# Four layers on one core: hybrid mixers and output products in one block, the fourth layer's retention beside its input products

## The chip, the cores and the metric

The kernel runs on one core of a Trainium2 chip. The metric is the time of one execution on the device in microseconds (us). The engines of the core are TensorE (PE; its weight loads are shown as PEld), VectorE (DVE), ScalarE (ACT), GpSimd (POOL) and SyncE (SP, which here issues DMAs). PSUM has eight banks of 512 float32 columns for TensorE's results.

## What is computed

Two blocks of two layers each work on 256 tokens of width 1024, in float32. The first two layers mix by convolution, sparse attention, linear attention and a gated MLP. The third layer (`hyb`) runs a gated delta rule and stick-breaking attention side by side, the fourth (`ret`) retention:

```python
def hybrid_mixer(h, ...):
    ...
    o_a = gated_delta_rule(qa, ka, va, g, beta)
    o_a = rms_norm_2(o_a, gdn_norm) * jax.nn.silu(_heads(gate, GDN_HEADS).astype(f32))
    ...
    o_b = stick_breaking_attention(qb, kb, vb)
    o = jnp.concatenate([_merge(o_a), _merge(o_b)], axis=-1).astype(h.dtype)
    return o @ w_out

def retention_mixer(h, w_in, w_out):
    ...
    o = retention_chunkwise(q, k, v)
    o = rms_norm_2(o) * jax.nn.silu(_heads(rg, RET_HEADS).astype(f32))
    return _merge(o).astype(h.dtype) @ w_out
```

Each mixer's result is scaled and added to x; a gated feed-forward part follows in each layer.

## The kernel before

All weights come as one stream of slots of 1 MB (128 partitions x 2048 columns) through a ring of six. SyncE issues the loads in the order of `plan()`. A slot is either modulation weights, which VectorE multiplies by the condition (`mod_sums`, L443), or weights of a product. For a product each float32 weight is split into a high and a low part, in two halves of 1024 columns: ScalarE copies the high part (`split_hi`, L425), VectorE subtracts it for the low part (`split_lo`, L432). The buffers `weights_hi_lo` hold two slots, so a split can begin when the slot two before it has been multiplied. TensorE then does three products for each pair of tiles (high by high, low by high, high by low): 48 products of 256 columns a slot, 24 a half.

Input products (`gemm_phase`, L537) take 15 slots in the hybrid layer and 24 in the fourth. ScalarE takes each finished bank two slots later in its queue (`evac`). Foreign work can be laid between slots: generators for each engine (`beside`) are advanced by one `yield` after each slot, so it all stands in the in-order queues of the engines, behind one split and ahead of the next. Output products (`rows_gemm_phase`, L836) need their activations split too, which GpSimd does (`split_acts`, L763 and L765) into `acts_hi_lo`. `rows_half` (L780) does half a slot of output products by itself; the first two layers use it in their mixers' stage.

An `nc.Block` is a piece of the program; all engines meet where it ends. One block holds layers 0 and 1 and the inputs of layer 2. Then come, each in a block of its own: `hyb_mixers`; the outputs and feed-forward part of layer 2 with the inputs of layer 3; `ret_phase`; the rest.

`hyb_mixers` is a chain of small products with VectorE in between: decays (first their broadcast, L1975), scores, a triangular inverse by doubling (L2014, L2021, L2024), then four steps of the recurrence (L2046 to L2062) with updates on VectorE (L2149 to L2163). The attention's outputs are copied to `oT` by ScalarE (L2229) during the recurrence. The delta outputs are then squared, normed, multiplied by gain and gate (L2169 to L2171), turned (L413) and copied. `ret_phase` computes scores (L2327), multiplies by the decays (L2293), multiplies by the values (L2335, four heads by two token tiles), norms rows of tokens (L2312, L2300), turns 32 blocks (L413) and copies them. The rotations of its q and k run on GpSimd beside the input slots.

## Time and profile before

| | us |
|---|---|
| median of 3 executions | 1613.58 |
| lowest, highest | 1611.7, 1614.3 |
| the profiled execution, its own time | 1613.15 |
| span of its trace, first to last instruction | 1611.4 |

The mean granted TensorE clock over the span is 0.95, as a share of 2.4 GHz: 1.00, or 0.50 for 1.2 GHz. The trace names instructions by line. A float32 product is recorded as two instructions, so 16 products of L2327 stand as x32; the products of split parts and the transposes are recorded once each. "[6.83 <-DVE arena L2171]" is the time that the engine sat idle before the first of these, and what released it. Times of a timeline count from the span's start.

### The profile page before, as it was taken

The numbers are of one execution on the slowest core, as the hardware profiler recorded it, in microseconds if no ns is written. First come the engines' busy times: TensorE is split into PE (matmuls) and PEld (weight loads), VectorE is DVE, ScalarE is ACT, GpSimd is POOL, SyncE is SP. The second block draws the span as 40 slices with busy tenths as digits, with TensorE's granted clock in tenths as the row PEclk, the third lists the DMA queues.
The fourth block names the chain that finished last, engine by engine and source line by source line (L and its number), as shares of the span: only waits on it lengthen the run. The fifth ranks groups of instructions, "written<-read, shape, count | busy, mean of one in ns | idle before, by whom it ended". The sixth has DMA issues, their size and how long they took to land. (4 is left out here: it accounts for less than half of the span.)

```text
span 1611.4 us, 28191 instructions
## 1 busy us (share of the span) xinstructions
PE 1516.3 (94%) x12038; PEld 1485.3 (92%) x12038; DVE 1084.0 (67%) x1451; ACT 750.0 (47%) x1016; POOL 412.4 (26%) x395
## 2 busy tenths in 40 slices
PE   4999899998999999999997879999999997999998
PEld 4999899998998999998997869999999996999998
DVE  7878597796557497796766556776468754465544
ACT  3545465434646365434775234444354443354432
POOL 0123020693121020594001220200329502220022
PEclk9998799998999799998999979999989998999999
DMA  9773389795341469796441004877548771446550
GB/s 395 308 300 139 111 306 343 284 340 203 115 191 63 153 257 360 284 341 221 154 171 43 1 33 147 318 288 262 183 160 294 269 270 53 183 162 218 215 192 27
DMA packets 47212, 336.69 MB, mean 209 GB/s; under 512 B 5360, under 2 KB 5744, under 8 KB 6768
## 3 DMA queue, kind: packets, MB, share of 16 engines
q1 hardware_dynamic: 46224, 333.03, 55.5%
q8 instruction: 95, 1.56, 0.4%
q10 hardware_dynamic: 864, 1.87, 0.3%
q14 instruction: 29, 0.24, 0.0%
HBM read 333.83 MB, written 1.05 MB: 208 GB/s over the span
## 5 line engine op out<-in xcount | busy, mean ns | idle before, releaser
L432 DVE TENSOR_TENSOR weights_hi_lo<-ring,weights_hi_lo 128x1024 fp32r<-128x1024 f32 x426 | 552.3, 1319 | 302.9 <-ACT weights_hi_lo L425 301.8
L425 ACT ACTIVATE weights_hi_lo<-ring 128x1024 fp32r<-128x1024 f32 x426 | 444.4, 1058 | 501.5 <-PE PS L537 277.8
L537 PE MATMUL PS<-hi,weights_hi_lo 128*128 128x256 f32 x3200 | 522.5, 286 | 14.5 <-ACT hi L652 12.4
L537 PEld LDWEIGHTS PS<-hi,weights_hi_lo 128*128 128x128 f32 x3200 | 447.4, 194 | 17.9 <-issue 14.8
L836 PE MATMUL PS<-acts_hi_lo,weights_hi_lo 128*128 128x256 f32 x3264 | 396.4, 284 | 8.2 <-DVE weights_hi_lo L432 8.0
L836 PEld LDWEIGHTS PS<-acts_hi_lo,weights_hi_lo 128*128 128x128 f32 x3264 | 392.8, 191 | 9.3 <-issue 8.6
L763 POOL CAST acts_hi_lo<-arena 128x256 fp32r<-128x256 f32 x144 | 135.6, 942 | 835.7 <-PE PS L836 419.9
L537 PE MATMUL PS<-lo,weights_hi_lo 128*128 128x256 f32 x1600 | 324.7, 285 | 0.0
L443 DVE CUSTOM_DVE_ANT_0 ring<-ring,cond 128x1024 f32<-128x1024 f32 x192 | 253.6, 1359 | 0.0
L537 PEld LDWEIGHTS PS<-lo,weights_hi_lo 128*128 128x128 f32 x1600 | 251.4, 193 | 0.0
L537 PE MATMUL PS<-weights_hi_lo,hi 128*128 128x256 f32 x1248 | 203.5, 285 | 1.2 <-ACT hi L652 1.2
L537 PEld LDWEIGHTS PS<-weights_hi_lo,hi 128*128 128x128 f32 x1248 | 172.0, 189 | 3.1 <-issue 2.9
L765 POOL TENSOR_TENSOR acts_hi_lo<-arena,acts_hi_lo 128x256 fp32r<-128x256 f32 x144 | 168.7, 1171 | 11.5
L537 PE MATMUL PS<-weights_hi_lo,lo 128*128 128x256 f32 x624 | 125.9, 283 | 0.0
L537 PEld LDWEIGHTS PS<-weights_hi_lo,lo 128*128 128x128 f32 x624 | 97.0, 190 | 0.0
L609 PEld LDWEIGHTS PS<-constS,arena 128*128 128x128 f32 x384 | 62.8, 254 | 12.7 <-ACT arena L644 11.8
L609 PE MATMUL PS<-constS,arena 128*128 128x1 f32 x384 | 63.2, 292 | 10.7 <-ACT arena L644 9.9
L2187 POOL TENSOR_TENSOR arena<-arena,constS 128x1024 f32<-128x1024 f32 x6 | 12.3, 2062 | 146.6 <-DVE arena L2115 136.5
L652 ACT ACTIVATE hi<-spare,mods 128x256 fp32r<-128x256 f32 x64 | 31.7, 507 | 31.1 <-DVE spare L663 31.1
L644 ACT ACTIVATE arena<-X 128x512 f32<-128x512 f32 (+1 forms) x40 | 21.7, 545 | 45.1 <-PE PS L609 22.0
L780 PE MATMUL PS<-acts_hi_lo,weights_hi_lo 128*128 128x256 f32 x288 | 39.7, 299 | 2.3 <-DVE heads L1592 2.1
L780 PEld LDWEIGHTS PS<-acts_hi_lo,weights_hi_lo 128*128 128x128 f32 x288 | 38.0, 205 | 2.9 <-DVE heads L1592 2.5
(349 smaller groups left out, 1117.9 us busy)
## 6 DMA issues: line engine op xcount, KB each, us to landing
ring<-in_stream_dram SPq DMA_DIRECT2D x313, 1024.0 KB, 4.9
constS<-in_const_dram SPq DMA_DIRECT2D x1, 1856.0 KB, 8.6
cond<-in_rows_dram SPq DMA_DIRECT2D x2, 512.0 KB, 5.2
arena<-in_x_dram ACTq DMA_DIRECT2D x1, 1024.0 KB, 11.3
smallS<-in_small_dram SPq DMA_DIRECT2D x1, 883.0 KB, 13.4
out_dram<-arena ACTq DMA_DIRECT2D x2, 256.0 KB, 2.5
out_dram<-arena SPq DMA_DIRECT2D x2, 256.0 KB, 3.3
constS<-in_const_dram SPq DMA_DIRECT2D x1, 320.0 KB, 14.7
```

The source lines that it names most:

```text
L425: act.activation(wsp[:, g % 2, 0, at:at + HALF], ring[:, n % RING, at:at + HALF], ACT.Copy).then_inc(*ready.one())
L432: dve.tensor_tensor(wsp[:, g % 2, 1, at:at + HALF], ring[:, n % RING, at:at + HALF], wsp[:, g % 2, 0, at:at + HALF].bitcast(F32), ALU.subt ...
L443: ins = dve.tensor_tensor_reduce(w[:, r, :], w[:, r, :], cond[:, 0 if q < 12 else 1, :], 1.0, 0.0, ALU.mult, ALU.add, mods[:, q, k:k + 1])
L537: mm = pe.matmul(o, lhs, rhs, start=k + g + j == 0, stop=k == KD - 1 and j == 2, skip_group_check=True)
L609: mm = pe.matmul(PS[:, bank, m:m + 1], sq[:, u % 2, c * SEQ + m * P:c * SEQ + (m + 1) * P], ones[:, 0:1], start=u + c + m == 0, stop=u == ...
L644: act.activation(sq[:, u % 2, 0:len(tiles) * SEQ], X[:, tiles[0]:tiles[-1] + 1, :].rearrange("p k t -> p (k t)"), ACT.Square).then_inc(*xs ...
L652: act.activation(hi[:, k, :], tmp[:, k % 4, :], ACT.Identity, bias=mods[:, q, k:k + 1]).then_inc(*hd.one())
L763: pool.tensor_copy(asp[:, a % 2, 0, g, :], src).then_inc(*acts_hi.one())
L765: pool.tensor_tensor(asp[:, a % 2, 1, g, :], src, asp[:, a % 2, 0, g, :].bitcast(F32), ALU.subtract).then_inc(*acts_lo.one())
L780: mm = pe.matmul(y_of(k), w[:, g, k * P:(k + 1) * P], x[:, g, :], start=fresh and g + j == 0 and (k % 2 == 0 or k == KD - 1), stop=False, ...
L836: mm = pe.matmul(y_of(k), w[:, g, k * P:(k + 1) * P], x[:, g, :], start=fresh and i + g + j == 0 and (k % 2 == 0 or k == KD - 1), stop=i = ...
L2187: pool.tensor_tensor(CT[v % 2], LT, cst(f"level{v}").unsqueeze(1).broadcast_to((P, 8, P)), ALU.mult).then_inc(*ctd.one())
```

## The change

1. `hyb_mixers` runs in the block of the inputs, and waits for single signals of the inputs' stage instead of the block's end. Its buffers are laid out anew: matrices of the triangular inverse and the decayed keys lie in idle halves of `weights_hi_lo`, in the order in which they come free for splits.
2. The hybrid layer's output slots come in the order 4, 6, 0, 2 (attention rows first). The first two are multiplied in `hyb_mixers` by `rows_half`, three halves ahead of the turns of the delta outputs and the fourth behind them, into banks 0 to 4. The first two turned blocks are split by ScalarE and VectorE straight from PSUM. The output phase goes on with the other two slots.
3. `ret_phase` is gone. Scores, decays, the products with the values, the norm and the gate are generators beside the fourth layer's input slots. The products with the values are done the other way round (channels on partitions), so nothing has to be turned. For the norm VectorE adds squares to one tile, TensorE sums it by a column of ones and spreads the roots. Gates are kept for two slots only and multiplied at once. The inputs use three banks instead of four, and the first output slot's weights are split in the inputs' stage (`split_weights=True`).
4. All of it is one block.

`split_hi` and `split_lo` take an argument for the halves to do. In the diff `slots` are the first two output slots, `following` the third.

```diff
-    return [("rows", name, i, k, 0) for k in ((4, 6, 0, 2) if kind == "mix" else range(0, chunks, 2))]
+    return [("rows", name, i, k, 0) for k in ((4, 6, 0, 2) if kind != "ret" else range(0, chunks, 2))]
...
+        if kind == "hyb":
+            phases.append((("mixed", l), merge(outs[:2], ("mixed", l))))
+            outs = outs[2:]
...
+            split_at = [[SPLIT_AT + 2 * SLOT * (product_no[n] % 2) + HALF * i for i in range(4)] for n in slots]
+            (hi0, hi1, lo0, lo1), (next_hi0, next_hi1, _, next_lo1) = split_at
+            decT, LT, T_, U_, W_ = (area(a, 8, P) for a in (7184, 8208, 9232, 10256, 11280))
+            CT = [area(a, 8, P) for a in (hi0, hi1)]
+            kbT, vb, kg, kdec, egb = (area(a, 8, P) for a in (lo0, lo1, next_hi0, next_hi1, next_lo1))
...
+                pe.wait_ge(*tka.at(4))
+                rows_half(pe, slots[0], 0, y_of, fresh=True)
+                rows_half(pe, slots[0], 1, y_of, fresh=True)
+                rows_half(pe, slots[1], 0, y_of, fresh=False)
+                pe.wait_ge(*onr.at(1))
+                transposes(pe, lambda i: og[:, i % 2, i // 2 * P:i // 2 * P + P], 8, 6, ft)
+                rows_half(pe, slots[1], 1, y_of, fresh=False)
...
+                exponents(4)
+                split_lo(dve, slots[0], (0,))
+                dve.wait_ge(*up_.at(1))
+                split_lo(dve, slots[0], (1,))
+                dve.wait_ge(*wp_.at(1))
+                dve.tensor_copy(wT, bank2(4)).then_inc(*wts.one())
...
+                            dve.wait_ge(*sts.at(n + 1))
+                            split_lo(dve, slots[1], (n - 1,))
...
+                split_lo(dve, following[0])
+                dve.wait_ge(*ft.at(1))
+                dve.wait_ge(acts_hi.sem, 2 * last + 2)
+                for g in range(2):
+                    dve.tensor_tensor(asp[:, last % 2, 1, g, :], PS[:, 6, g * SEQ:(g + 1) * SEQ],
+                                      asp[:, last % 2, 0, g, :].bitcast(F32), ALU.subtract).then_inc(*acts_lo.one())
...
+                for i in range(2):
+                    split_acts(pool, oT[:, 4 + 2 * i:6 + 2 * i, :], slots[i:i + 1], ready=[tka.at(3 + i)] * 2)
...
+                split_hi(act, slots[0], (0,))
+                act.wait_ge(*up_.at(1))
+                act.activation(u, bank2(2), ACT.Copy).then_inc(*us.one())
+                split_hi(act, slots[0], (1,))
+                for g in range(2):
+                    act.wait_ge(*dif.at(4 * g + 4))
+                    act.activation(Zs[g], Zs[g], ACT.Exp).then_inc(*av.one())
+                act.wait_ge(*wp_.at(1))
+                split_hi(act, slots[1], (0,))
+                for b in range(2):
+                    if b:
+                        act.wait_ge(*kvs.at(3))
+                        split_hi(act, slots[1], (1,))
...
+                split_hi(act, following[0])
+                act.wait_ge(*ft.at(1))
+                act.wait_ge(acts_lo.sem, 2 * last)
+                for g in range(2):
...
+                if i >= 18:
+                    act.wait_ge(*gated.at(i - 17))
+                return act.activation(gates[:, i % 2, :], bank, ACT.Silu)
...
+                gemm_phase(blk, ("proj", l), lambda i: 256 if 8 <= i < 16 else 0, evac, banks=3, split_weights=True,
+                           beside=retention(QK, V, gates))
+            return proj, None, QK
...
+            score_at, out_at = {10: 0, 12: 1, 13: 2, 15: 3}, {12: 0, 14: 1, 18: 2, 19: 3}
...
+            def pe_beside(pe):
+                for i in range(24):
+                    if i in score_at:
+                        h = score_at[i]
+                        pe.wait_ge(*rot_done.at(h + 5))
+                        if h:
+                            pe.wait_ge(*at_.at(h))
                         for kt in range(TT):
                             for c in range(2):
+                                mm = pe.matmul(PS[:, 3, 256 * kt:256 + P * kt], QK[:, 8 + 2 * h + c, kt * P:(kt + 1) * P],
                                                QK[:, 2 * h + c, kt * P:SEQ], start=c == 0, stop=c == 1)
                         mm.then_inc(*ap_.one())
+                    if i in out_at:
+                        h = out_at[i]
+                        pe.wait_ge(*at_.at(h + 1))
+                        pe.wait_ge(*taken.at(10 + 2 * h))
+                        if h >= 2:
+                            pe.wait_ge(*yn.at(2 * h - 2))
+                        o = pair_banks(h)
+                        for c in range(4):
+                            for kt in range(TT):
+                                mm = pe.matmul(o[:, c, kt * P:SEQ], V[:, kt, h * 512 + c * P:h * 512 + (c + 1) * P],
+                                               att[:, h, 256 * kt:256 + P * kt], start=kt == 0 and c % 2 == 0, stop=kt == 1,
+                                               skip_group_check=True)
                         mm.then_inc(*op.one())
+                    if i in (16, 21):
+                        g = 0 if i == 16 else 1
+                        pe.wait_ge(*at_.at(4))
+                        if g:
+                            pe.wait_ge(*yn.at(4))
+                        for h in (2 * g, 2 * g + 1):
+                            pe.wait_ge(*ad.at(h + 1))
+                            for m in range(TT):
+                                mm = pe.matmul(PS[:, 3, 2 * (h % 2) + m:2 * (h % 2) + m + 1], sq[:, h % 2, m * P:(m + 1) * P],
+                                               ones[:, 0:1], start=h % 2 + m == 0, stop=True, skip_group_check=True)
+                        mm.then_inc(*gsum.one())
+                    if i in (17, 22):
+                        g = 0 if i == 17 else 1
+                        pe.wait_ge(*grc.at(g + 1))
+                        for j in range(4):
+                            mm = pe.matmul(PS[:, 3, j * P:(j + 1) * P], r[:, 4 * g + j:4 * g + j + 1].to_broadcast((P, P)), ident,
+                                           start=j == 0, stop=True, skip_group_check=True)
+                        mm.then_inc(*gsp.one())
+                    yield
+            def act_beside(act):
+                for i in range(25):
+                    for h, at in ((0, 14), (1, 16), (2, 20), (3, 21)):
+                        if i == at:
+                            act.wait_ge(*op.at(h + 1))
+                            if h:
+                                act.wait_ge(*ad.at(h))
+                            if h >= 2:
+                                act.wait_ge(*yn.at(4))
+                            for b in range(2):
+                                act.activation(squares(h, b), pair_banks(h)[:, 2 * b:2 * b + 2, :], ACT.Square).then_inc(*gsq.one())
+                    if i in (17, 22):
+                        g = 0 if i == 17 else 1
+                        act.wait_ge(*gsum.at(g + 1))
+                        act.activation(r[:, 4 * g:4 * g + 4], PS[:, 3, 0:4], ACT.Sqrt, bias=cst("eps"), scale=1.0 / 512).then_inc(*grt.one())
+                    if i in (18, 23):
+                        act.wait_ge(*gsp.at(1 if i == 18 else 2))
+                        act.activation(sq[:, 0, :], PS[:, 3, :], ACT.Copy).then_inc(*rsb.one())
+                    yield
...
+            def dve_beside(dve, order):
+                for i in range(28):
+                    for h, at in ((0, 11), (1, 13), (2, 14), (3, 16)):
+                        if i == at:
+                            dve.wait_ge(*ap_.at(h + 1))
+                            dve.tensor_tensor(att[:, h, :], PS[:, 3, 0:384], dec[:, h, :], ALU.mult).then_inc(*at_.one())
+                    for h, at in ((0, 14), (1, 16), (2, 20), (3, 21)):
+                        if i == at:
+                            a, b = squares(h, 0), squares(h, 1)
+                            dve.wait_ge(*gsq.at(2 * h + 2))
+                            order(dve.tensor_tensor(a, a, b, ALU.add))
+                            dve.tensor_tensor(a[:, 0, :], a[:, 0, :], a[:, 1, :], ALU.add).then_inc(*ad.one())
+                    if i in (17, 22):
+                        g = 0 if i == 17 else 1
+                        dve.wait_ge(*grt.at(g + 1))
+                        dve.reciprocal(r[:, 4 * g:4 * g + 4], r[:, 4 * g:4 * g + 4]).then_inc(*grc.one())
+                    if i in (18, 23):
+                        g = 0 if i == 18 else 1
+                        dve.wait_ge(*rsb.at(g + 1))
+                        dve.wait_ge(*ap_.at(4))
+                        for h in (2 * g, 2 * g + 1):
+                            for b in range(2):
+                                v = sq[:, 0, h % 2 * 256:h % 2 * 256 + 256].unsqueeze(1).broadcast_to((P, 2, SEQ))
+                                dve.tensor_tensor(yT[:, 4 * h + 2 * b:4 * h + 2 * b + 2, :], pair_banks(h)[:, 2 * b:2 * b + 2, :], v,
+                                                  ALU.mult).then_inc(*yn.one())
+                    n = i - 19
+                    if 0 <= n < 8:
+                        dve.wait_ge(*taken.at(17 + n))
+                        dve.wait_ge(*yn.at(n + 1))
+                        v = yT[:, 2 * n:2 * n + 2, :].rearrange("p k t -> p (k t)")
+                        dve.tensor_tensor(v, v, gates[:, n % 2, :], ALU.mult).then_inc(*gated.one())
+                    yield
...
+            inputs, mixers, mixed = layers[2]
+            inputs(blk)
+            mixers(blk)
+            outputs(blk, 2, mixed, acts_split=1, acts_ready=[state.pop("mixed")] * 4, fresh=False, y_banks=(0, 1, 2, 3, 4))
+            ffn_phases(blk, 2)
+            layers[3][0](blk)
+            outputs(blk, 3, layers[3][2], acts_ready=state.pop("gated"))
```

TensorE at the end of the hybrid layer, before (L2046 to L2062 are the recurrence's last step, L413 the turns, L836 the output products, L609 sums of the next norm; a branch ends a block or phase):

```order
L2046 MATMUL PS<-arena 64x128 x4
L2050 MATMUL PS<-arena 64x128 x4
L2062 MATMUL PS<-arena 64x128 x4
L413 MATMUL PS<-constS,arena 128x128 x8
L1932 UNCONDITIONAL_BRANCH
L815 UNCONDITIONAL_BRANCH
L836 MATMUL PS<-acts_hi_lo,weights_hi_lo 128x256 x192
L609 MATMUL PS<-constS,arena 128x1 x16
```

And of the change (L2077 to L2093 are the last step, L786 `rows_half`, L416 the turns, L846 the output phase, L615 the next norm):

```order
L2077 MATMUL PS<-arena 64x128 x4
L2081 MATMUL PS<-arena 64x128 x4
L2093 MATMUL PS<-heads 64x128 x4
L786 MATMUL PS<-acts_hi_lo,weights_hi_lo 128x256 x72
L416 MATMUL PS<-constS,arena 128x128 x8
L786 MATMUL PS<-acts_hi_lo,weights_hi_lo 128x256 x24
L823 UNCONDITIONAL_BRANCH
L846 MATMUL PS<-acts_hi_lo,weights_hi_lo 128x256 x96
L615 MATMUL PS<-constS,arena 128x1 x16
```

72 output products stand ahead of the turns and 24 behind them; one branch is gone.

VectorE between the inverse and the recurrence's state updates, before (L2088 exponents of the attention, L2141 the copy of w, L2149 and L2152 values of v, L2159 and L2163 state updates):

```order
L2088 TENSOR_TENSOR heads<-heads,PS 128x384 x2
L2088 TENSOR_TENSOR spare<-spare,PS 128x384 x2
L2141 COPY arena<-PS 128x1024
L2088 TENSOR_TENSOR spare<-spare,PS 128x384 x2
L2149 COPY arena<-arena 64x4x128
L2159 COPY arena<-PS 128x512
L2152 TENSOR_TENSOR arena<-arena,PS 64x4x128
L2163 SCALAR_TENSOR_TENSOR arena<-arena,PS 128x128 x4
L2152 TENSOR_TENSOR arena<-arena,PS 64x4x128
```

And of the change (L2124, L2180, L2188, L2191, L2198 and L2202 are the same work, L438 is `split_lo`):

```order
L2124 TENSOR_TENSOR spare<-spare,PS 128x384 x2
L438 TENSOR_TENSOR weights_hi_lo<-ring,weights_hi_lo 128x1024 x2
L2180 COPY arena<-PS 128x1024
L2124 TENSOR_TENSOR spare<-spare,PS 128x384 x2
L2188 COPY heads<-arena 64x4x128
L2198 COPY arena<-PS 128x512
L2191 TENSOR_TENSOR heads<-arena,PS 64x4x128
L2202 SCALAR_TENSOR_TENSOR arena<-arena,PS 128x128 x4
L438 TENSOR_TENSOR weights_hi_lo<-ring,weights_hi_lo 128x1024
L2191 TENSOR_TENSOR heads<-arena,PS 64x4x128
```

Two split pieces now stand ahead of the copy of w, and one behind the state update shown (one more behind the next).

ScalarE at the end of the fourth layer's inputs, before (L2248 takes a gate's bank, L2312 and L408 are `ret_phase`; the splits, L425, stand between the rows of L2248):

```order
L2248 ACTIVATE arena<-PS 128x2x256 x3
L2421 UNCONDITIONAL_BRANCH
L2307 UNCONDITIONAL_BRANCH
L2312 ACTIVATE arena,stat<-PS 128x512 x4
L408 ACT_TABLE_LOAD
L408 ACTIVATE stat<-stat 128x4
L2312 ACTIVATE arena,stat<-PS 128x512 x4
```

And of the change (L429 is `split_hi`, L2314 takes a gate's bank, L2415 are the roots, L2418 the copy of the spread roots):

```order
L2415 ACT_TABLE_LOAD
L2415 ACTIVATE stat<-PS,constS 128x4
L429 ACTIVATE weights_hi_lo<-ring 128x1024 x2
L2314 ACT_TABLE_LOAD
L2314 ACTIVATE arena<-PS 128x512
L2418 ACTIVATE arena<-PS 128x512
L2314 ACTIVATE arena<-PS 128x512
L429 ACTIVATE weights_hi_lo<-ring 128x1024 x2
L2314 ACTIVATE arena<-PS 128x512
L869 UNCONDITIONAL_BRANCH
L429 ACTIVATE weights_hi_lo<-ring 128x1024 x16
```

The roots and the copy stand between splits, and the split of the first output slot stands behind the last bank but one.

VectorE at the same place, before (L432 is `split_lo`, L2293 the decays of `ret_phase`):

```order
L457 TENSOR_TENSOR mods<-mods,smallS 128x8
L432 TENSOR_TENSOR weights_hi_lo<-ring,weights_hi_lo 128x1024 x2
L2421 UNCONDITIONAL_BRANCH
L2287 UNCONDITIONAL_BRANCH
L2293 TENSOR_TENSOR arena<-PS,constS 128x384 x4
L400 TENSOR_SCALAR stat<-stat 128x4
```

And of the change (L462 and L463 end a modulation, L438 is `split_lo`, L2448 multiplies by the roots, L2455 by the gates):

```order
L462 SCALAR_TENSOR_TENSOR mods<-mods,smallS 128x8
L463 TENSOR_TENSOR mods<-mods,smallS 128x8
L438 TENSOR_TENSOR weights_hi_lo<-ring,weights_hi_lo 128x1024 x2
L2448 TENSOR_TENSOR arena<-PS,arena 128x512 x4
L2455 TENSOR_TENSOR arena<-arena 128x512
L438 TENSOR_TENSOR weights_hi_lo<-ring,weights_hi_lo 128x1024 x2
L2455 TENSOR_TENSOR arena<-arena 128x512 x3
L888 UNCONDITIONAL_BRANCH
L438 TENSOR_TENSOR weights_hi_lo<-ring,weights_hi_lo 128x1024 x16
```

Four root products and a gate product stand between the split of the last input slot and that of the first output slot.

## Rows read from the trace of the kernel before

**Rows 1.** Page, part 1: busy time, share of the span, instructions.

```profile
PE 1516.3 (94%) x12038; PEld 1485.3 (92%) x12038; DVE 1084.0 (67%) x1451; ACT 750.0 (47%) x1016; POOL 412.4 (26%) x395
```

**Rows 2.** Windows; PE, PEld, DVE, ACT, POOL busy; clock; DMA share; GB/s.

```profile
947.10:960.00 12.90, 1.97 (x8) 1.59 (x9) 8.25 (x10) 5.21 (x6) 2.60 (x4) 0.57 0.00 1
960.00:985.60 25.60, 25.60 (x195) 25.60 (x195) 14.78 (x16) 8.84 (x10) 9.98 (x13) 0.88 0.53 192
1329.60:1359.90 30.30, 21.16 (x88) 14.47 (x89) 12.75 (x22) 12.77 (x27) 2.59 (x4) 0.92 0.00 1
```

**Rows 3.** PE timeline, fourth layer (start us, us, what, idle before, its releaser).

```profile
1328.46 0.40 PE L537 MATMUL PS<-weights_hi_lo,lo 128*128 128x256 f32 x2
...
1329.18 0.40 PE L537 MATMUL PS<-weights_hi_lo,lo 128*128 128x256 f32 x2
...
1330.58 5.48 PE L2327 MATMUL PS<-arena 128*128 128x256 f32 x32 [1.00 <-PEq L2421]
...
1335.89 10.47 PE L2335 MATMUL PS<-arena 128*128 128x512 f32 x24
...
1359.91 48.09 PE L836 MATMUL PS<-acts_hi_lo,weights_hi_lo 128*128 128x256 f32 x384 [3.86 <-DVE weights_hi_lo L432]
```

**Rows 4.** The same timeline, hybrid layer's mixers and its output products.

```profile
861.45 2.03 PE L1975 MATMUL PS<-constS,stat 128*128 128x128 f32 x16
...
953.91 1.97 PE L413 MATMUL PS<-constS,arena 128*128 128x128 f32 x8 [6.83 <-DVE arena L2171]
...
960.00 25.61 PE L836 MATMUL PS<-acts_hi_lo,weights_hi_lo 128*128 128x256 f32 x192 [4.12 <-DVE weights_hi_lo L432]
```

**Rows 5.** ScalarE's timeline, from the hybrid inputs to its output products.

```profile
859.18 0.60 ACT L1721 ACTIVATE arena<-PS 128x512 f32<-128x512 f32 x1 [4.10 <-PE PS L537]
...
926.85 1.02 ACT L2223 ACTIVATE arena<-PS 128x1024 f32<-128x1024 f32 x1 [6.81 <-PE PS L2031]
...
944.36 0.60 ACT L2229 ACTIVATE arena<-PS 128x512 f32<-128x512 f32 x1 [4.69 <-PE PS L1967]
...
965.56 1.06 ACT L425 ACTIVATE weights_hi_lo<-ring 128x1024 fp32r<-128x1024 f32 x1 [4.36 <-PE PS L836]
```

**Rows 6.** VectorE's timeline, end of the hybrid layer's recurrence and its norm.

```profile
928.64 1.23 DVE L2141 COPY arena<-PS 128x1024 f32<-128x1024 f32 x1 [3.02 <-PE PS L2034]
929.78 1.15 DVE L2088 TENSOR_TENSOR spare<-spare,PS 128x384 f32<-128x384 f32 x2
930.84 0.41 DVE L2149 COPY arena<-arena 64x512 f32<-64x512 f32 x1
...
945.24 0.69 DVE L2152 TENSOR_TENSOR arena<-arena,PS 64x512 f32<-64x512 f32 x1 [2.27 <-PE PS L2046]
...
952.63 1.22 DVE L2171 TENSOR_TENSOR arena<-arena 128x1024 f32<-128x1024 f32 x1
```

**Rows 7.** GpSimd's timeline, splits of activations beside output products.

```profile
960.39 1.39 POOL L763 CAST acts_hi_lo<-arena 128x256 fp32r<-128x256 f32 x1
...
961.86 1.59 POOL L765 TENSOR_TENSOR acts_hi_lo<-arena,acts_hi_lo 128x256 fp32r<-128x256 f32 x1
```

**Rows 8.** VectorE's timeline, a modulation piece and a split, fourth layer's inputs.

```profile
1314.58 1.22 DVE L443 CUSTOM_DVE_ANT_0 ring<-ring,cond 128x1024 f32<-128x1024 f32 x1
...
1319.19 1.23 DVE L432 TENSOR_TENSOR weights_hi_lo<-ring,weights_hi_lo 128x1024 fp32r<-128x1024 f32 x1 [0.58 <-ACT weights_hi_lo L425]
```

**Rows 9.** Timelines: sums by a column, table change, four multiplies of 512.

```profile
747.33 0.95 PE L609 MATMUL PS<-constS,arena 128*128 128x1 f32 x8
...
1342.28 1.28 ACT L408 ACT_TABLE_LOAD   x1 [0.28 <-DVE stat L400]
...
1347.89 2.73 DVE L2300 SCALAR_TENSOR_TENSOR arena<-PS,stat,arena 128x512 f32<-128x512 f32 x4
```

**Rows 10.** Waits of PE, second layer, 450 to 600 us: total, times, longest.

```profile
PE PS L780 <- DVE heads L1592: 1.2, 1, 1.2
```

**Rows 11.** Windows again, columns as in Rows 2, first layer's mixers.

```profile
150.00:154.00 4.00, 4.00 (x21) 3.94 (x19) 4.00 (x7) 2.42 (x3) 4.00 (x1) 0.52 0.79 276
```

717 lines of the change are left out of this document (336 added, 381 removed).

## Prediction

> **What bounds the kernel now.** I read the page first: TensorE is busy 94% of the span [rows 1], so time can only come from stretches in which it idles, runs at half clock, or does work that could go. The windows by stretch show two such places, one in each of the last two layers. After the hybrid layer's recurrence TensorE works 1.97 us out of 12.90 at a mean granted clock of 0.57, and the output products behind it start at the lower level (mean 0.88) [rows 2]. In the fourth layer 30.3 us lie between the input products and the output products, with DMA at rest [rows 2]. TensorE's own timeline then says what ended each wait.
>
> Pace: six of the large products start 0.72 us apart [rows 3], so 0.12 us each at 2.4 GHz, a slot of 48 takes 5.76 us and half a slot 2.88.
>
> **Part 1, the hybrid layer.** Where TensorE stood before, in order of time.
>
> (a) The broadcasts of g stand behind a block boundary and start at 861.45 [rows 4]. In the new order there is no boundary. The broadcasts wait only for the last bank to be taken, by the ScalarE copy that starts at 859.18 and takes 0.60 [rows 5], so they start near 859.85. VectorE's masks of the decays wait for TensorE's transposes behind these broadcasts, so the whole stage moves: gain 1.6.
>
> (b) Two split pieces are put into VectorE's queue ahead of the copy of w (L2141). VectorE's second piece waits for ScalarE's: ScalarE copies u from 926.85 to 927.87, then splits 1.06, to 928.95 [rows 5]; VectorE then needs 1.23 [rows 8], to 930.2. Behind it stand the copy of w, two exponents and the copy of v, which before began at 928.64 and ended at 931.25 [rows 6]: 2.6 us, now from 930.2 to 932.9. The recurrence waits for just these: loss 1.7. The other two pieces go into VectorE's waits between the state updates, 2.27 us where I see one [rows 6], and cost 1.23: hidden, if ScalarE's half is there.
>
> (c) Recurrence to output products. Before: the recurrence's last product ends at 947.08 (953.91 - 6.83), TensorE waits 6.83 for the norm, the gain and the gate on VectorE (to 953.85), turns eight blocks in 1.97, waits 4.12 for a boundary and a first split, then does 192 products in 25.61 [rows 4, 6]. Now three halves, 72 products of 8.64 us, need no delta output. Their weights are split in (b); their activations are attention copies, the last of which ScalarE ends at 944.96 [rows 5]. GpSimd splits them at no more than 1.4 and 1.6 us a piece [rows 7], four pieces a slot: the second slot's are there by 951 and wanted from 952.7 on. So the 6.83 is covered by products, with 1.8 to spare; the turns, at full clock, take about half of 1.97; the fourth half (2.88) covers the copy and split of the turned blocks, two ScalarE and two VectorE pieces. Gains: 6.83 (the wait), 4.12 (the boundary and the first split), 1.0 (the turns at full clock), and 25.61 - 192 x 0.12 = 2.6 (the products at full clock).
>
> Sum of part 1: 1.6 - 1.7 + 6.8 + 4.1 + 1.0 + 2.6 = **14.4**.
>
> **Part 2, the fourth layer.** Removed from TensorE's path: all from the end of the inputs (1330.58 - 1.00 = 1329.58) to the first output product (1359.91), 30.3 us [rows 3], and the half-clock start of 384 output products, 48.09 - 46.08 = 2.0 [rows 3].
>
> Added to TensorE between input slots, one after the other with them:
> - scores, the same 16 products: 1335.89 - 1330.58 = 5.3 [rows 3];
> - outputs turned, 16 products of 256 and 16 of 128 columns. Before they were 12 of 512 in 10.47: 6144 columns both times, so 10.5 [rows 3];
> - sums of squares by a column of ones, eight products: four take 0.95, so 1.9 [rows 9];
> - spreading the roots, eight products of 128: the same shape takes 2.03 for eight, so 2.0 [rows 4].
> Gone without replacement: 32 transposes, the row-wise norm, the barrier and the cold split. Sum added 19.7.
>
> Waits: the rest is laid beside 24 slots. VectorE gets four decays, four pairs of adds, eight multiplies by the root and eight by the gate: at 0.69 each at most, some 18 us in a stage that TensorE lengthens by 19.7. Each of these stands in VectorE's or ScalarE's queue behind one split and ahead of the next, so a late one delays the next slot's weights. I followed the queues slot by slot and find one place where the lead runs out. Count from the end of slot 22. TensorE spreads the roots (1.0), and does slot 23 until 6.8. VectorE has just done a modulation piece (2 x 1.22 and small ones) and slot 23's split (2 x 1.23), and is free at 2.2 [rows 8]. It then owes four multiplies (2.73 [rows 9]), to 4.9, and a gate (0.69), to 5.6. ScalarE may take bank 22 only after that gate, since there are two gate buffers: 6.2. Then it splits the next weights, first half to 7.3, and VectorE the low part to 8.5. TensorE wants them at 6.8: 1.7, with semaphore hops 2.0. For all other places I take 0.5 in all: in the second layer, built in the same way, TensorE's longest wait for such a piece is 1.2 [rows 10]. Bounds for all waits: 0 to 8.
>
> Gain of part 2: 30.3 + 2.0 - 19.7 - 2.5 = **10.1** (bounds 4.6 and 12.6).
>
> ScalarE changes tables in that chain, for the root and back for the gate's Silu. A change takes 1.28 here [rows 9], and at that both are done before TensorE or VectorE could wait for them longer than I have counted. The Trainium skill, "ScalarE: Activation LUTs", section "Table sets: the hidden batching unit", gives about 2.7 us for one; by that the last stall would grow by up to 2 x 1.4 and the forecast be some 1592. The row decides.
>
> Extra DMA or semaphores: the stream has the same slots, in another order for the hybrid outputs; DMA runs at 192 GB/s beside the output products [rows 2] and is not pressed. The ring's prefetch is hidden by TensorE's full slots before and behind.
>
> **Sum.** 14.4 + 10.1 = 24.5 off the profiled execution's 1613.15 gives 1588.6; that execution lies 0.4 under the median of 1613.58, so 1589.
>
> **Rivals.**
> (R1) Only the hybrid layer gains. The queues of the fourth layer lose at several slots what the pause cost: some 10 us in 14 slots, 0.7 each. For it: nearly every slot from 10 on has a piece of foreign work, and VectorE waits in its queue for TensorE's result each time. Against: the second layer's waits [rows 10]. Time: 1613.6 - 14.4 = 1599. Chance 0.11.
> (R2) Slower. In-order queues lose their one-slot lead at every slot from 10 to 23, and TensorE then sees ScalarE's and VectorE's split in full, 1.06 + 1.23 = 2.3, 14 times: 32 us. Part 2 is then 12.6 - 32 = -19.6, the whole 14.4 - 19.6 = -5.2: 1619. It decides from stalls of 27 us in all, 1.9 a slot. Against: the pieces beside one slot are well under the 5.76 of it. Chance 0.03.
> (R3) The clock falls where I count full pace. After the wait of 6.8 it was at half. But it also stood at 0.52 from 150 to 154 us, when TensorE was busy 4.00 of 4.00 us with thin products of 64 columns [rows 11]. The new sums (one column) and the 1.7 of (b) are such places: three of them, at 2.6 each as in the outputs, give 1597. Chance 0.12. The Trainium skill, "TensorE: Matmul & The Clock Gate", section "HAM oscillation — how this bites in real kernels", ties the fall to pauses of TensorE; by that rule only (b) could be hit, 1591.6, and the fourth layer would keep its clock. The row at 150 us shows a fall without a pause, so I keep this case.
> (R4) The change doesn't do what it says in the hybrid layer: the three halves wait for GpSimd's splits or the banks, so the products stay behind the norm. Then the 6.8 stays: 1596. Against: by the durations in (c) both slots' pieces are there before they are wanted. Chance 0.06.
> (R5) Better than forecast: (b) and the stalls hidden, 1589 - 4 = 1585. It lies inside the forecast's own range.
>
> **How the numbers follow.** Forecast 0.68, with its own range of 1583 to 1594 (R5's end, and waits of 7 instead of 2.5). The range that should hold 8 in 10 reaches up over R3, R4 and R1, and down to 1582, where a 14.4 of 16 and a 10.1 of 13 or more would be needed: 1582 to 1600. A measurement of this kernel tells about 0.2% (3 us) from no change. All cases but R2 are faster by more. Faster 0.95, same 0.02, slower 0.03.
>
> **What would show it.** Right: no idle of TensorE over 1 us between the recurrence's last product and the hybrid layer's next norm, and its clock at 1.00 there; recurrence about as late as before; the fourth layer's output products start within 3 us of the last input product, at clock 1.00; input stage about 22 us longer. Wrong: product waits for split weights at slots 11 to 23, or a clock of 0.50 in the input stage of the fourth layer or behind the copy of w; a wait of the fourth half for the turned blocks. What would make the sum wrong most is a queue order in VectorE that I took to be covered.

## The result and the profile after

The changed kernel takes **1589.4 us** (median of 1586.94, 1589.38 and 1593.05) against 1613.25 for the kernel before (median of four). The ratio of the means is 0.9855, 95% interval 0.983 to 0.9881, or 23.4 us less. Two executions in a slower state of the chip are left out here and below: one of the changed kernel (1671.7 us at a mean granted clock of 0.82; with it the median is 1591.2) and one of the kernel before (2130.4 us at 0.64). Two more series of the same kernel, further down, gave ratios of 0.983 (0.9812 to 0.9848) and 0.9835 (0.9815 to 0.9855). All eleven times lie between 1582.7 and 1593.1 with a median of 1586.9, against a median of 1613.1 for 34 of the kernel before: 26 us less. The prediction was 1589, 24.5 less, in a range of 1582 to 1600.

That spread of 10 us is the first thing to explain, and one stretch of the profile turns out to account for about half of it. The profile is of the slowest of these executions (1593.05, span 1591.2). First TensorE's timeline from the hybrid layer's inputs to its next norm (start in us, us, what, idle before and what ended it), which answers to [rows 4]. Here L2003 is the broadcast of g, L2086 and L2077 to L2093 the recurrence (with the attention's products, L1990, laid between), L786 the halves of the output products, L416 the turns, L846 the rest of the products:

```profile
860.19 2.02 PE L2003 MATMUL PS<-constS,stat 128*128 128x128 f32 x16 [0.43 <-ACT arena L1731]
...
930.71 1.13 PE L2086 MATMUL PS<-heads,arena 64*128 64x128 f32 x8 [2.35 <-DVE heads L2188]
...
933.52 1.97 PE L2077 MATMUL PS<-arena 128*64 128x128 f32 x8
935.28 1.91 PE L2081 MATMUL PS<-arena 128*64 128x128 f32 x8
...
950.82 1.04 PE L2081 MATMUL PS<-arena 128*64 128x128 f32 x8
...
952.80 8.78 PE L786 MATMUL PS<-acts_hi_lo,weights_hi_lo 128*128 128x256 f32 x72
961.42 1.04 PE L416 MATMUL PS<-constS,arena 128*128 128x128 f32 x8
962.21 3.08 PE L786 MATMUL PS<-acts_hi_lo,weights_hi_lo 128*128 128x256 f32 x24
965.12 11.52 PE L846 MATMUL PS<-acts_hi_lo,weights_hi_lo 128*128 128x256 f32 x96
976.48 4.36 PE L615 MATMUL PS<-constS,arena 128*128 128x1 f32 x32
```

Behind the recurrence everything is as forecast: no row has a wait in brackets. The 6.83 and the 4.12 of [rows 4] are gone, the turns take 1.04 instead of 1.97, and from the recurrence's end to the norm's first sum it is 23.7 us (952.80 to 976.48) where it was 38.4 (947.08 to 985.45). Inside the recurrence something is wrong: the same four products (eight rows of L2081) take 1.91 us at 935 and 1.04 at 951. The windows name it (busy time of PE, PEld, DVE, ACT, POOL; granted clock; DMA share; GB/s):

```profile
931.00:945.00 14.00, 14.00 (x71) 12.02 (x70) 3.73 (x7) 2.29 (x3) 0.40 (x1) 0.53 0.10 40
...
953.00:962.00 9.00, 9.00 (x78) 9.00 (x78) 7.55 (x8) 4.55 (x5) 0.16 (x1) 1.00 0.13 54
962.00:976.00 14.00, 14.00 (x121) 14.00 (x119) 7.96 (x12) 6.54 (x9) 4.20 (x4) 1.00 0.53 183
```

For 14 us TensorE works without a pause at its lower level, 1.2 GHz, behind a wait of 2.35 us. From the first product of the recurrence to the first half it takes 22.09 us; at full clock, as we shall see, 15.61. So this execution pays 6.48 us there. VectorE's timeline shows where the 2.35 come from, and answers to [rows 6] (L438 are the low parts of split weights, L2180 the copy of w, L2188 the copy of v; two exponents lie between):

```profile
923.56 1.22 DVE L438 TENSOR_TENSOR weights_hi_lo<-ring,weights_hi_lo 128x1024 fp32r<-128x1024 f32 x1
926.95 1.23 DVE L438 TENSOR_TENSOR weights_hi_lo<-ring,weights_hi_lo 128x1024 fp32r<-128x1024 f32 x1 [2.17 <-ACT weights_hi_lo L429]
928.09 1.22 DVE L2180 COPY arena<-PS 128x1024 f32<-128x1024 f32 x1
...
930.15 0.41 DVE L2188 COPY heads<-arena 64x512 f32<-64x512 f32 x1
...
958.43 1.23 DVE L2212 TENSOR_TENSOR arena<-arena 128x1024 f32<-128x1024 f32 x1
```

The second piece waits for ScalarE and holds back the copy of w. The last row is the gate behind the norm: it ends at 959.66, and TensorE comes to the turns only at 961.42, so the halves cover the chain with 1.8 us to spare, as predicted.

The fourth layer, from the scores (L2365) over outputs (L2377), sums of squares (L2389) and spreads (L2396) to the output products (L846); what lies between are input products. It answers to [rows 3]:

```profile
1259.90 1.47 PE L2365 MATMUL PS<-arena 128*128 128x256 f32 x8
1261.20 2.78 PE L2377 MATMUL PS<-later,arena 128*128 128x256 f32 x16
...
1327.24 0.95 PE L2389 MATMUL PS<-constS,arena 128*128 128x1 f32 x8
...
1333.76 1.05 PE L2396 MATMUL PS<-constS,stat 128*128 128x128 f32 x8
...
1341.61 45.69 PE L846 MATMUL PS<-acts_hi_lo,weights_hi_lo 128*128 128x256 f32 x384 [1.09 <-DVE weights_hi_lo L438]
1387.14 4.91 PE L615 MATMUL PS<-constS,arena 128*128 128x1 f32 x32
```

and the windows there (the first holds the whole stage behind its start, the second the output products):

```profile
1200.00:1341.00 141.00, 140.51 (x1152) 139.06 (x1150) 100.33 (x116) 62.92 (x78) 64.34 (x51) 1.00 0.65 240
1341.00:1387.00 46.00, 45.39 (x383) 45.42 (x384) 27.77 (x28) 18.67 (x20) 15.54 (x24) 1.00 0.54 197
```

Of a gap of 30.3 us one wait of 1.09 is left, at full clock. The span is 20.2 us shorter: the first of the next norm's sums comes 9.0 us earlier in the hybrid layer (976.48 against 985.45), of which 0.9 are lost again ahead of the fourth layer (its inputs start 8.1 us earlier, 1181.99 against 1190.07; in the 23.5 us from the first sum on the granted clock was 0.78 against 0.85). The fourth layer gains 12.6, and some 0.5 is lost behind it.

### The profile page after: what moved, and what is told of

Read it like the earlier page. It is cut to its first block, busy times and chain, and to the rows that moved or that the text cites. A ratio compares the mean times of both kernels' runs of the same rounds, so it can differ in the third digit from the quotient of the medians.

```text
span 1591.2 us, 28263 instructions
## 1 busy us (share of the span) xinstructions
PE 1513.8 (95%) x12078; PEld 1487.8 (94%) x12078; DVE 1086.8 (68%) x1461; ACT 750.8 (47%) x1011; POOL 406.1 (26%) x391
## 4 chain that ended last, share of the span: by engine, by line
PE 74%; issue 11%; POOL 8%; DVE 5%; ACT 1%; DMA 0%; ACTq 0%; POOLq 0%; DVEq 0%
PE PS L543 44%; PE PS L846 14%; POOL acts_hi_lo L769 4%; POOL acts_hi_lo L771 4%; PE PS L786 3%; PE PS L615 2%; DVE ring L449 2%; PE PS L1078 1%; PE PS L2377 1%; PE PS L1456 1%; PE PS L623 1%; PE PS L2055 1%; PE PS L1436 1%; DVE weights_hi_lo L438 1%; PE PS L1464 1%
## 5 line engine op out<-in xcount | busy, mean ns | idle before, releaser
L438 DVE TENSOR_TENSOR weights_hi_lo<-ring,weights_hi_lo 128x1024 fp32r<-128x1024 f32 x426 | 550.9, 1317 | 272.8 <-ACT weights_hi_lo L429 271.4
L429 ACT ACTIVATE weights_hi_lo<-ring 128x1024 fp32r<-128x1024 f32 x426 | 444.5, 1058 | 477.4 <-PE PS L543 270.1
L543 PE MATMUL PS<-hi,weights_hi_lo 128*128 128x256 f32 x3456 | 562.2, 285 | 14.1 <-ACT hi L658 12.1
L543 PEld LDWEIGHTS PS<-hi,weights_hi_lo 128*128 128x128 f32 x3456 | 480.5, 193 | 17.5 <-issue 14.6
L846 PE MATMUL PS<-acts_hi_lo,weights_hi_lo 128*128 128x256 f32 x3168 | 379.8, 281 | 1.3 <-DVE weights_hi_lo L438 1.1
L846 PEld LDWEIGHTS PS<-acts_hi_lo,weights_hi_lo 128*128 128x128 f32 x3168 | 376.4, 189 | 2.0 <-issue 1.3
L543 PE MATMUL PS<-lo,weights_hi_lo 128*128 128x256 f32 x1728 | 349.8, 284 | 0.0
L543 PEld LDWEIGHTS PS<-lo,weights_hi_lo 128*128 128x128 f32 x1728 | 270.6, 193 | 0.0
L543 PE MATMUL PS<-weights_hi_lo,hi 128*128 128x256 f32 x992 | 162.5, 286 | 1.2 <-ACT hi L658 1.2
L543 PEld LDWEIGHTS PS<-weights_hi_lo,hi 128*128 128x128 f32 x992 | 137.2, 190 | 3.1 <-issue 2.9
L543 PE MATMUL PS<-weights_hi_lo,lo 128*128 128x256 f32 x496 | 100.0, 283 | 0.0
L543 PEld LDWEIGHTS PS<-weights_hi_lo,lo 128*128 128x128 f32 x496 | 77.2, 190 | 0.0
L615 PEld LDWEIGHTS PS<-constS,arena 128*128 128x128 f32 x384 | 62.0, 251 | 12.5 <-ACT arena L650 11.6
L615 PE MATMUL PS<-constS,arena 128*128 128x1 f32 x384 | 62.4, 290 | 10.7 <-ACT arena L650 9.9
L786 PE MATMUL PS<-acts_hi_lo,weights_hi_lo 128*128 128x256 f32 x384 | 50.9, 293 | 2.0 <-DVE heads L1602 2.0
L786 PEld LDWEIGHTS PS<-acts_hi_lo,weights_hi_lo 128*128 128x128 f32 x384 | 48.8, 198 | 2.6 <-DVE heads L1602 2.4
```

The lines of the kernel that those rows point to most:

```text
L429: act.activation(wsp[:, g % 2, 0, at:at + HALF], ring[:, n % RING, at:at + HALF], ACT.Copy).then_inc(*ready.one())
L438: dve.tensor_tensor(wsp[:, g % 2, 1, at:at + HALF], ring[:, n % RING, at:at + HALF], wsp[:, g % 2, 0, at:at + HALF].bitcast(F32), ALU.subt ...
L543: mm = pe.matmul(o, lhs, rhs, start=k + g + j == 0, stop=k == KD - 1 and j == 2, skip_group_check=True)
L615: mm = pe.matmul(PS[:, bank, m:m + 1], sq[:, u % 2, c * SEQ + m * P:c * SEQ + (m + 1) * P], ones[:, 0:1], start=u + c + m == 0, stop=u == ...
L786: mm = pe.matmul(y_of(k), w[:, g, k * P:(k + 1) * P], x[:, g, :], start=fresh and g + j == 0 and (k % 2 == 0 or k == KD - 1), stop=False, ...
L846: mm = pe.matmul(y_of(k), w[:, g, k * P:(k + 1) * P], x[:, g, :], start=fresh and i + g + j == 0 and (k % 2 == 0 or k == KD - 1), stop=i = ...
```

## The experiments

Each run stood beside runs of the kernel before on its own chip, and three chips were used. "Less" and "more" with an interval come from the ratio of the means to the kernel before on the same chip; a plain difference of medians can lie some 3 us away from it. Four things were to be settled: what each part gives alone; whether the half clock in the recurrence comes from the longer wait; whether the cover of the norm is what gains in the hybrid layer; and what the last wait in the fourth layer is.

**The same kernel again** (two runs, on two chips). No edit.

> The changed kernel once more, unaltered, as the ruler for the others on this chip. Theory A (the clock falls in the recurrence in some executions only, as its profile had it at 0.53 over 931 to 945 us for about 6.4 us): times from about 1585 to 1593, scattered over several us, and the profile shows the recurrence either from 930.7 to about 946.4 at 1.00 or to 952.8 at half clock. Theory B (the clock always falls there, since the waits ahead of it are always the same): the recurrence ends 22 us after it began in this profile too, and the times lie around 1590 with the scatter of the kernel before, some 2.5 us.

Measured: 1584.8 (1582.7 to 1587.4). Its profile has the same wait, but a short fall:

```profile
928.09 1.13 PE L2086 MATMUL PS<-heads,arena 64*128 64x128 f32 x8 [2.35 <-DVE heads L2188]
...
931.58 1.91 PE L2081 MATMUL PS<-arena 128*64 128x128 f32 x8
...
945.32 8.79 PE L786 MATMUL PS<-acts_hi_lo,weights_hi_lo 128*128 128x256 f32 x72
```

The recurrence takes 17.23 us (928.09 to 945.32), 1.62 over full pace, instead of 6.48: neither of the two ends that the expectation named, but between them. Theory A in kind: the fall's length changes from one execution to the next with the program unchanged. That it can be nothing was not seen.

> The changed kernel unaltered, beside the next three on one chip. From its seven undisturbed times so far (1582.7 to 1593.1): a median between 1584 and 1590, with a spread of 4 us or more. If the half clock in the recurrence comes and goes, the profile shows it again at another length than the 14 and the 4 us seen so far, or not at all.

Measured: 1586.9 (1583.6 to 1589.2); recurrence 17.23 again (932.93 to 950.16). The expected spread is there. The spread of the times is not all from this place: in this profile the broadcast of g starts 3.6 us later than in the one before (860.56 against 856.95), so something ahead of it moves too.

**The parts alone.** The fourth layer's functions of the kernel before put into the changed one, and the reverse:

```
-            layers[3][0](blk)
-            outputs(blk, 3, layers[3][2], acts_ready=state.pop("gated"))
+            layers[3][0](blk)
+        layers[3][1]()
+        with block() as blk:
+            outputs(blk, 3, layers[3][2])
```

> Part one of the change alone: the hybrid layer as changed, the fourth layer's retention in a block of its own behind its inputs, as before. By the sum of the prediction 14.4 us less than the kernel before (about 1599), with the clock at half through the recurrence 6 less gained, 8 to 9 us (about 1604). If the parts add up, it stands 10 to 12 us above the changed kernel in the same runs.

Measured: 1600.4 (1590.1 to 1602.7, six times), ratio 0.991 (0.9886 to 0.9934): 14.5 us less (10.6 to 18.4). It stands 12.9 above the changed kernel on the same chip by the ratios, 15.7 by the medians, where 10 to 12 were expected. Its profile, of the slowest of the six, has the long fall: wait of 2.34, recurrence of 22.09 (930.38 to 952.47).

> Part two of the change alone: the hybrid layer as in the kernel before, the fourth layer's retention beside its inputs as changed. By the sum of the prediction 10.1 us less than the kernel before; by the profile of the changed kernel, whose only wait there is 1.1 us where 2.5 were put down, 11 to 12 less, so about 1601 to 1603. Rival (the parts help each other, since one block of the program is left between them less): clearly under 10, with the rest only where both are there.

Measured: 1601.5 (1600.5 to 1601.8), ratio 0.9925 (0.9913 to 0.9937): 12.1 us less (10.2 to 14.0). The parts add up within these intervals: 14.5 + 12.1 = 26.6, against 26 for the whole over all series. The rival in which they help each other, with part two clearly under 10, is out. So is, with its interval, the case that only the hybrid layer gains. This kernel has the recurrence of the kernel before with its wait of 1.07, and its profile shows that a short fall can come there too:

```profile
932.46 1.13 PE L2058 MATMUL PS<-arena 64*128 64x128 f32 x8 [1.07 <-DVE arena L2152]
...
934.53 1.90 PE L2049 MATMUL PS<-arena 128*64 128x128 f32 x8
936.22 1.91 PE L2053 MATMUL PS<-arena 128*64 128x128 f32 x8
938.06 1.16 PE L2058 MATMUL PS<-arena 64*128 64x128 f32 x8
```

**The split pieces late.** VectorE's side only:

```
-                split_lo(dve, slots[0], (0,))
-                dve.wait_ge(*up_.at(1))
-                split_lo(dve, slots[0], (1,))
...
                             dve.tensor_copy(new, kv).then_inc(*sts.one())
+                            split_lo(dve, slots[0], (0,))
...
-                            split_lo(dve, slots[1], (n - 1,))
+                            split_lo(dve, slots[n - 1], (2 - n,))
...
                 dve.tensor_tensor(og, og, GT, ALU.mult).then_inc(*onr.one())
+                split_lo(dve, slots[1], (1,))
```

> VectorE's pieces of the split move out of the stretch ahead of the recurrence: the first output slot's two go behind the first and second state update, the second slot's first behind the third, its last behind the gated outputs. ScalarE's side stays. The wait of TensorE ahead of the recurrence should fall from 2.35 us to about 1.1, as in the kernel before. Theory A (the longer wait brought the clock down for the recurrence): 1.3 us from the wait and up to 6.4 from the clock, so 2 to 8 us less than the changed kernel, about 1583 to 1588, with the recurrence at 1.00. Theory B (the clock falls at the phase that the stage has by then, whatever this wait is): only about 1.3 us less, and the recurrence at 0.5 all the same. Rival: the moved pieces come too late for the fourth half or for the next slot, and 1 to 2 us come back there as waits.

Measured: 1584.2, four times within 1583.8 to 1585.3.

```profile
932.03 1.13 PE L2086 MATMUL PS<-heads,arena 64*128 64x128 f32 x8 [1.07 <-DVE heads L2185]
...
934.10 1.09 PE L2077 MATMUL PS<-arena 128*64 128x128 f32 x8
935.03 1.04 PE L2081 MATMUL PS<-arena 128*64 128x128 f32 x8
...
947.64 8.79 PE L786 MATMUL PS<-acts_hi_lo,weights_hi_lo 128*128 128x256 f32 x72
```

The wait is 1.28 shorter, as wanted, the recurrence runs at full pace in 15.61 us, and no late piece makes TensorE wait behind it. The median, though, is only 0.5 under the changed kernel on the same chip (1584.8, with the short fall in its profile), so the 2 to 8 us of theory A did not come. The four times spread by 1.5 us against 4.8, but that is not shown to be the edit's doing: the two kernels below that have the late pieces and one more edit each, in the fourth layer or at the block's end, spread by 8.9 and 6.7.

**The wait filled.** Eight products of the unit matrix, which nobody reads:

```
                 later_sums(6)
+                for _ in range(8):
+                    pe.matmul(PS[:, 0, 0:P], ident, ident, start=True, stop=True)
                 pe.wait_ge(*wts.at(1))
```

> The changed kernel with eight 128x128 fp32 products of the unit matrix, whose result nobody reads, put into bank 0 ahead of TensorE's wait for the recurrence: at 0.22 us each they fill 1.8 of its 2.35 us and delay nothing. Theory A (the clock fell because TensorE stood idle there): the recurrence runs at 1.00, up to 6.4 us less than the changed kernel where that has the fall, median 2 to 6 less; the wait shown is 0.5. Theory B (the fall has another cause, earlier in the stage): no change in time within 1 us, and the recurrence at 0.5 as before.

Measured: 1588.4 (1581.1, 1588.2, 1588.5, 1588.8). Theory A wanted a median 2 to 6 us less; it is 3.6 more than the changed kernel's on this chip. The profile is of the fastest, 1581.1, and there the recurrence is as theory A has it, with VectorE's work unchanged and the wait down to 0.56:

```profile
926.73 1.95 PE L2069 MATMUL PS<-constS 128*128 128x128 f32 x16
929.23 1.13 PE L2088 MATMUL PS<-heads,arena 64*128 64x128 f32 x8 [0.56 <-DVE heads L2190]
...
944.85 8.78 PE L786 MATMUL PS<-acts_hi_lo,weights_hi_lo 128*128 128x256 f32 x72
```

15.62 us. But the three other times are all above the changed kernel's highest there (1587.4), and no trace says where they lost it. As a remedy this is not shown.

**The wait lengthened.** The kernel with the late pieces, with the copy of w made three times:

```
                 dve.wait_ge(*wp_.at(1))
+                order(dve.tensor_copy(wT, bank2(4)))
+                order(dve.tensor_copy(wT, bank2(4)))
                 dve.tensor_copy(wT, bank2(4)).then_inc(*wts.one())
```

> The kernel with the late pieces (1584.2), and VectorE makes its copy of w three times instead of once, which only lengthens TensorE's wait ahead of the recurrence, from 1.07 to about 3.5 us (2 x 1.22). Theory A (the longer wait brings the clock down for the recurrence): 2.4 from the wait and 1.5 to 6.4 from the clock, so 4 to 9 us more, and half clock in the recurrence in the profile. Theory B (the order of the pieces, not the wait, made the difference): 2.4 us more, with the recurrence at 1.00.

Measured: 1594.2 (1580.6 to 1597.8, six times), 10.0 over the median of the kernel with the late pieces on another chip. The wait itself grew by 2.37. The fall is in the profile:

```profile
926.00 1.78 PE L2086 MATMUL PS<-heads,arena 64*128 64x128 f32 x8 [3.44 <-DVE heads L2187]
...
931.36 1.90 PE L2081 MATMUL PS<-arena 128*64 128x128 f32 x8
933.19 1.16 PE L2086 MATMUL PS<-heads,arena 64*128 64x128 f32 x8
```

It costs 3.23 us there (18.84 from 926.00 to 944.84). So theory B's recurrence at 1.00 is out for this execution; but three of seven profiles with the wait of 1.07 have a short fall too (table below), so one profile doesn't show that the length of the wait brought it. The profiled execution is at the same time the fastest of the six. Its granted clock was 1.00 from 876 to 892, where the changed kernel has 0.79 to 0.85, which can be why. The times don't decide either: the medians leave 7.6 over the wait, the ratios (0.9868 with 0.9838 to 0.9897, against 0.9827 with 0.9811 to 0.9842) leave 4.2 with an uncertainty of some 5, and the five slower executions have no trace. Theory A is likely, not shown.

**More filling**, here and at the norms, on the kernel with the late pieces and the early split (below):

```
+                        if h0 < 6:
+                            for _ in range(7):
+                                pe.matmul(PS[:, 2, 0:P], ident, ident, start=True, stop=True)
                         pe.wait_ge(*dif.at(h0))
```

> The kernel with the late pieces and the early split in the fourth layer (1581.9 on another chip), and idle products of the unit matrix (128x128 fp32, 0.22 us each) in three waits of the hybrid stage: seven in each of the two of 1.80 us ahead of the later sums, four in the 1.07 us ahead of the recurrence. Theory A (TensorE's idle time there brings the clock down in the recurrence): no half clock between 905 and 960 us, the scatter of the times stays under 3 us, and the median 0 to 2 us under that kernel. Theory B (the falls come from further ahead in the program): falls and scatter as before, and a median within 1 us of it. Rival: the seven take longer than the wait, and 0.5 to 1 us is lost.

Measured: 1584.8 (1580.6 to 1586.1), 2.1 under the changed kernel on this chip. Its base is on another chip; against the kernel before the two have 0.9824 and 0.9817, so no gain over it is seen. Full clock from 905 to 960 us in the profile, as theory A has it (15.61 for the recurrence), and still a spread of 5.5 in the times, as theory B has it. Clock falls elsewhere (0.87 from 876 to 892 in this profile) may make it; which place makes it was not traced.

```
                     unit_sums(pe, u, sq, 0, xsq, xsum)
+                for _ in range(3):
+                    pe.matmul(PS[:, 1, 0:P], ident, ident, start=True, stop=True)
                 spread(pe, r, 2, xr, rx)
+                for _ in range(5):
+                    pe.matmul(PS[:, 1, 0:P], ident, ident, start=True, stop=True)
```

> The same kernel as base (1581.9 on another chip), and idle products of the unit matrix beside every norm of X: three (0.7 us at full clock) in the wait for the root, five (1.1) in the wait for the first scaled tile. In the profiles the input products behind each norm run at half clock for some 5 us, which costs about half of that at each of eight places. If the idle 0.6 and 1.2 us are what brings the clock down: half clock goes from the first products of each stage, up to 8 x 2.7 = 21 us less. If the thin sums ahead of them (32 products of one column, in which TensorE counts as busy) have brought it down by then: the fillers run at half clock themselves, take 0.44 us each, 3.5 us together against the 1.8 idle, and 8 x 1 to 1.7 = 8 to 13 us are lost.

Measured: 1584.2 (1582.2 to 1587.5). Neither 21 gained nor 8 lost. The norm behind the hybrid layer, first without, then with the fillers (L617 sums, L645 and L648 fillers, L625 spread, L543 input products):

```profile
970.26 3.95 PE L617 MATMUL PS<-constS,arena 128*128 128x1 f32 x32
...
976.67 1.19 PE L543 MATMUL PS<-hi,weights_hi_lo 128*128 128x256 f32 x4 [1.21 <-ACT hi L660]
...
982.86 0.63 PE L543 MATMUL PS<-hi,weights_hi_lo 128*128 128x256 f32 x4
```

```profile
972.13 4.87 PE L617 MATMUL PS<-constS,arena 128*128 128x1 f32 x32
976.86 1.63 PE L645 MATMUL PS<-constS 128*128 128x128 f32 x6
978.28 1.06 PE L625 MATMUL PS<-constS,stat 128*128 128x128 f32 x4
979.13 2.27 PE L648 MATMUL PS<-constS 128*128 128x128 f32 x10
981.13 0.75 PE L543 MATMUL PS<-hi,weights_hi_lo 128*128 128x256 f32 x4
...
984.80 0.63 PE L543 MATMUL PS<-hi,weights_hi_lo 128*128 128x256 f32 x4
...
988.07 0.73 PE L543 MATMUL PS<-hi,weights_hi_lo 128*128 128x256 f32 x4 [0.97 <-DVE weights_hi_lo L438]
```

At this norm the input products do start at full clock now, 0.75 for four against 1.19. The fillers ahead of them ran at half clock. From the first sum to the thirty-first product it is 12.60 us without and 12.67 with, but the sums, which stand ahead of all fillers, took 0.92 of that more in this execution (4.87 against 3.95): behind the sums 0.85 is gained. The stage, faster at its start, then waits 0.97 for VectorE's split, which the slow start had covered. So it goes at three norms that both traces show: from the first sum to the second slot's first product it is 14.71, 15.05 and 15.24 us without fillers and 15.94, 15.38 and 15.06 with them, and at the second of these the first four products are still at half clock (1.20). What the fillers gain, the wait for the split takes back.

**Turns first**, on the kernel with the late pieces: the wait for the gated outputs and the turns ahead of all four halves, so that nothing covers the norm.

```
+                pe.wait_ge(*onr.at(1))
+                transposes(pe, lambda i: og[:, i % 2, i // 2 * P:i // 2 * P + P], 8, 6, ft)
                 rows_half(pe, slots[0], 0, y_of, fresh=True)
```

> The kernel with the late pieces (1584.2), and the turns of the delta outputs put ahead of all four halves of the output products, so that nothing covers the norm's chain. If the cover is worth what the prediction says: TensorE waits 6.8 us for the gated outputs, and the clock at half for some us after it adds 1 to 3, so 7 to 10 us more, 1591 to 1594. Rival (the products fit in later at no loss, because something else is late): under 3 us more.

Measured: 1593.2 (1591.6 to 1595.2), 9.0 more than the median of its base on another chip. The traces say the same: from the recurrence's end to the norm's first sum it is 32.78 us (948.18 to 980.96) against 23.70 (947.64 to 971.34), 9.1 more.

```profile
955.10 1.94 PE L416 MATMUL PS<-constS,arena 128*128 128x128 f32 x8 [6.92 <-DVE arena L2210]
956.69 13.07 PE L786 MATMUL PS<-acts_hi_lo,weights_hi_lo 128*128 128x256 f32 x96
```

The wait is back with 6.92, the turns are at half clock, and so is the start of the products (13.07 for 96, where 72 and 24 took 8.79 and 3.08). That is the cover's price: the wait and 2.1 of clock.

**The block's end back** between the hybrid inputs and the delta stage, on the kernel with the late pieces.

```
             inputs(blk)
+        with block() as blk:
             mixers(blk)
```

> The kernel with the late pieces (1584.2), and the end of the block put back between the hybrid layer's input products and its delta stage, as in the kernel before. By the prediction's term this is worth 1.6 us, so 1585 to 1586, and in the profile 1.6 us more from the end of the input products to the broadcast of the gates' sums. Rival: nothing (under 0.5), because the stage would wait for the norm of the heads anyway.

Measured: 1585.0 (1584.1 to 1590.9), too near to tell by times. In the profile the broadcast starts 2.02 us after the start of the last two input products (860.98 to 863.00), 1.18 without the boundary (859.74 to 860.92): 0.84, neither the 1.6 of the term nor nothing. In the kernel before it is 2.70 (858.75 to 861.45), so from before to after 1.52 are gained. What made that kernel's boundary 0.68 dearer was not tried; it also had SyncE's wait for the layer's tables in it.

```profile
862.56 0.36 PE L1998 MATMUL PS<-stat,constS 128*128 128x8 f32 x2 [1.19 <-PEq L2520]
```

**The fourth layer's split first**, on the kernel with the late pieces:

```
+                if name == ("proj", 3):
+                    split_hi(act, following[0])
                 take(n_pe - 2)
```

> The kernel with the late pieces (1584.2), and in the fourth layer ScalarE splits the first output slot's weights ahead of its evacuation of the gate's seventh bank, which waits for a gate buffer. If that evacuation is what holds the split back, TensorE's wait of 1.09 us ahead of the fourth layer's output products goes, 1.1 us less, about 1583, which the profile can show and the times hardly. Rival (VectorE's own order holds it, which has the normed heads to write ahead of its half of the split): the wait stays between 0.5 and 1.1.

Measured: 1581.9 (1580.3, 1581.4, 1581.9, 1582.9, 1589.2), ratio to before 0.9817 (0.9798 to 0.9837). The wait is gone; first TensorE, then VectorE:

```profile
1330.92 14.25 PE L848 MATMUL PS<-acts_hi_lo,weights_hi_lo 128*128 128x256 f32 x119
```

```profile
1328.45 0.68 DVE L2456 TENSOR_TENSOR arena<-arena 128x512 f32<-128x512 f32 x1
1329.05 2.35 DVE L438 TENSOR_TENSOR weights_hi_lo<-ring,weights_hi_lo 128x1024 fp32r<-128x1024 f32 x2
```

VectorE splits right behind the gate, since ScalarE's half is there; before, it stood idle 1.67 us at this point for it. So ScalarE's order was the cause, and VectorE's own order was not. The kernel has the lowest median of all here, 1581.9, but its interval overlaps the changed kernel's, and the two never ran on the same chip.

All profiles of the recurrence together, from its first product to the first half (in the two kernels with the old order, to its end):

```
wait ahead   recurrence, us                    over full pace
0.17, 0.56   15.61, 15.62                      0, 0
1.07         15.6 or 15.7 four times,          0, 0, 0, 0,
             17.3, 17.23, 17.23                1.6, 1.6, 1.6
2.34, 2.35   22.09, 22.09, 17.23, 17.23        6.5, 6.5, 1.6, 1.6
3.44         18.84                             3.2
```

A short fall of 1.6 came with either wait; the long one was seen only behind 2.34 and 2.35, in two of four. Not every wait brings a fall: TensorE also waits twice for 1.80 us earlier in the stage (L1979), and the granted clock was 1.00 from 905 to 928 us in all three profiles of the changed kernel.

## Why the prediction came out right, and where it was off

The time was forecast for mostly the right reasons. Two errors offset each other, and that they did is luck: a fall of the clock in the hybrid layer that the sum left out, and a fourth layer that gained more than forecast.

**Part 1.** Forecast 14.4; alone it gave 14.5, with an interval of 8 us, so the terms must be read in the traces.
- (a) 1.6: the way from the last input products to the broadcast is 1.52 shorter. Right in size; the block's end by itself cost 0.84 where it was put back, and what the other 0.68 was stays open.
- (b) -1.7: the wait grew by 1.28 (2.35 against 1.07). The size is right. What the step left out is the clock behind it: the mean extra time in the recurrence is 4.0 us in four profiles of this order, 0.7 in seven of the shorter wait. This is the term that failed, -1.7 where in the first profile 1.28 + 6.48 = 7.8 were lost and in the next two 1.28 + 1.62 = 2.9. That the longer wait causes the long fall is the likeliest reading of the table, but these are few profiles, and no series of times shows it.
- (c) 6.83 + 4.12 + 1.0 + 2.6 = 14.5: the way from the recurrence's end to the norm is 38.37 - 23.68 = 14.7 shorter. Right, and the turns put first (9.1 back in the traces) show that the cover is the cause of most of it. The rest, the 4.12 of boundary and first split and what is left of the clock, was not taken out by itself.
- The two other pieces, called hidden: at 940.39 and 948.79 in VectorE's waits, at no cost. Right.

Sum by traces: 1.5 - 1.3 + 14.7 = 14.9 without a fall, 8.4 with the long one, 13.3 with the short one.

**Part 2.** Forecast 10.1 (bounds 4.6 and 12.6); alone 12.1 (10.2 to 14.0). By the profile, from the first input product to the first output product it is 169.84 us before (1190.07 to 1359.91) and 159.62 after (1181.99 to 1341.61), 10.2 less, and the output products are 2.4 shorter (47.93 to 45.53, from their start to the first sum): 12.6.
- Added work 19.7: the stage without its gap was 139.51 long (169.84 - 30.33), with the retention and up to its last input product 158.53: 19.0 added. Right.
- Half-clock start 2.0: measured 2.4. Right.
- Waits 2.5: 1.1, at the place and with the releaser foretold, and none elsewhere. Too high by 1.4; together with the two above, 2.5.

**The rivals.** R1 (only the hybrid layer gains) and R2 (the lead is lost at slot after slot) fall with TensorE's waits from 1165 to 1392 us: besides those at the two norms only the 1.1. R4 falls with rows that have no wait between 952.80 and 976.48. R3 is half true. Of its three places the two with thin sums kept their clock (1.00 from 1200 to 1341 us, over both), and the one of (b) lost it, at 1.6 to 6.5 instead of 2.6. The Trainium skill, "TensorE: Matmul & The Clock Gate", section "HAM oscillation — how this bites in real kernels", ties a fall to TensorE's pauses; by that rule only (b) could be hit. This case's traces agree as to the place: filled to 0.17 and 0.56 us the wait had no fall, at 2.35 always one. They don't say that the pause alone decides: at 1.07 three profiles of seven had a fall, at the two waits of 1.80 none did. They also show that the work behind the wait was a stage without idle time, and stayed at half clock for up to 14 us.

R5's thought, that (b) and the last stall could be hidden, was sound by the traces: the late pieces brought the first wait back to 1.07, and with the early split the last one is gone. Their kernel came to 1581.9, which the times don't separate from the changed kernel's.

**The signs.** No wait behind the recurrence, clock 1.00 there, output products 1.1 us behind the last input product, clock 1.00: all as listed. The input stage grew by 19.0, not by about 22. "Recurrence about as late as before" failed in the first profile: it ended at 952.80 against 947.08 (at 945.32 and 950.16 in the next two). The same list named "a clock of 0.50 behind the copy of w" as what would show it wrong, and that is what came. The total held because part 2 gave back 2.5 and because the long fall is not in every profile.

## What to carry to other kernels

Ahead of a serial stage of small products, price a longer wait of TensorE by itself and by what the clock may do behind it: here profiles with 1.3 us more of wait had a mean of 3.3 us more in the stage (4.0 in four profiles against 0.7 in seven), and the length of the fall, which differs between executions, is part of the scatter of a series. Work that is to be hidden belongs into the waits inside such a stage or behind it, not ahead of its first link, and where two engines make a piece together, look at the first one's order too (the last wait of the fourth layer went with one line of ScalarE's). Covering a serial chain by products that don't need it gains the wait and the clock behind it, 6.9 and 2.1 here; idle fillers gained nothing that the times could show, since the wait for the next split took back what they gained.

## What the runs showed of the hardware

- The granted clock can fall in a stretch in which TensorE is busy without a pause (14.00 of 14.00 us at 0.53), right behind a wait of 2.35 us, and the same program with the same wait lost 6.48 us there in one execution and 1.62 in another. Single profiles of this kernel differ by 5 us for this alone.
- The clock doesn't fall behind every wait: it was 1.00 over two waits of 1.80 us in the same stage.
- Fillers can bring the clock back before the real work (four products 0.75 us instead of 1.19, at one norm; 1.20 still at another), but themselves ran at half clock, nearly twice their full-clock time (2.27 for five, against 1.95 for eight at full clock).
